# Four weight splits and the columns moved in a fused two-block kernel's beginning, column sums closed by kind, splits and turnings moved in its last mixer

## The reference, cut to what matters

```
m_lat = silu(c)     @ ada_w[i] + ada_b[i]      # 6 parts of 1024: shift, scale, gate, twice
m_ctx = silu(c_ctx) @ ada_w[i] + ada_b[i]
h = rms_norm(x) * (1 + scale) + shift
x = x + gate * rms_norm(mixer(h));  x = x + gate * rms_norm(relu(h' @ w1)**2 @ w2)
```

```
s   = (q @ k.T) * exp(logd - m_t)              # logd: decays, masked
num = s @ v + w_inter * (q @ C);  den = sum(s) + w_inter * (q @ n)
out = num / max(|den|, exp(-m_t))              # then directions added, RMS norm by head
y   = (sigmoid(o) * out * norm_w) @ w_out
```

## Time and profile before

| | us |
|---|---|
| median of 3 runs (lowest, highest) | 2018.97 (2018.01, 2020.7) |
| profiled execution, its own time | 2022.0 |
| its span, first to last instruction | 2020.2 |
| TensorE busy | 1967.8 |
| VectorE busy | 1359.3 |
| ScalarE busy | 886.4 |
| mean granted TensorE clock | 0.989 |

### The profile page before, as it was taken

How to read it: one execution, slowest core, us unless ns; L and a number is a source line. 1 busy time by engine, 2 the same in 40 slices (tenths; PEclk the granted TensorE clock), 3 DMA queues, 4 the chain that set the end, 5 groups by cost and what they waited for, 6 DMA issues and landing times.

```text
span 2020.2 us, 27551 instructions
## 1 busy us (share of the span) xinstructions
PE 1967.8 (97%) x10390; PEld 1643.3 (81%) x10390; DVE 1359.3 (67%) x2172; ACT 886.4 (44%) x1513; POOL 254.4 (13%) x333
## 2 busy tenths in 40 slices
PE   7899999999999999999999999999999999989998
PEld 3777788888888777888998888878888878878897
DVE  4778777777756645487987675667655477667655
ACT  2523345232333544476554224624243354556554
POOL 2101011111110210411101000111011021331000
PEclk9889999999999999999999999999999999999999
DMA  8334226565664261258874432555555345236753
GB/s 290 117 100 119 90 70 212 188 178 159 193 181 139 93 201 53 83 185 284 262 229 139 156 105 71 188 170 168 152 168 165 86 133 179 89 101 217 229 184 114
DMA packets 191859, 315.20 MB, mean 156 GB/s; under 512 B 14653, under 2 KB 114328, under 8 KB 191728
## 3 DMA queue, kind: packets, MB, share of 16 engines
q1 hardware_dynamic: 162512, 210.09, 32.4%
q0 software_dynamic: 29216, 103.36, 17.1%
HBM read 312.35 MB, written 1.05 MB: 155 GB/s over the span
## 4 chain that ended last, share of the span: by engine, by line
PE 89%; DVE 4%; issue 2%; ACT 2%; POOL 1%; DMA 1%; SPq 0%; POOLq 0%; DVEq 0%; ACTq 0%
PE bank L676 26%; PE bank L683 24%; PE bank L682 24%; PE bank L686 11%; PE bank L681 2%; PE bank L679 2%; ACT junk L1556 1%; PE bank L745 1%; DVE wl L2153 1%; POOL st L3140 1%; DVE X L2275 0%; PE bank L1045 0%; DVE acc L2178 0%; ACT wh L1540 0%; ACT ta L1584 0%
## 5 line engine op out<-in xcount | busy, mean ns | idle before, releaser
L1540 ACT ACTIVATE wh<-raw 128x1024 fp32r<-128x1024 f32 (+4 forms) x390 | 399.3, 1030 | 602.0 <-PE bank L683 564.1
L2153 DVE TENSOR_TENSOR wl<-raw,wh 128x1024 fp32r<-128x1024 f32 (+3 forms) x372 | 440.0, 1189 | 297.3 <-ACT wh L1540 296.8
L676 PE MATMUL bank<-HH,wh 128*128 128x256 f32 (+1 forms) x1552 | 517.1, 333 | 2.8 <-issue 2.1
L682 PE MATMUL bank<-HL,wh 128*128 128x512 f32 (+1 forms) x1232 | 415.0, 337 | 0.0
L683 PE MATMUL bank<-HH,wl 128*128 128x512 f32 (+1 forms) x1232 | 415.0, 337 | 0.0
L2178 DVE SCALAR_TENSOR_TENSOR acc<-ada,sc,acc 128x512 f32<-128x512 f32 x518 | 362.3, 746 | 2.3
L676 PEld LDWEIGHTS bank<-HH,wh 128*128 128x128 f32 x1552 | 294.8, 190 | 32.5 <-issue 6.4
L676 PE MATMUL bank<-wh,UH 128*128 128x512 f32 x768 | 302.3, 394 | 0.0
L683 PE MATMUL bank<-wh,UL 128*128 128x512 f32 x768 | 301.4, 393 | 0.0
L682 PE MATMUL bank<-wl,UH 128*128 128x512 f32 x768 | 301.0, 392 | 0.0
L682 PEld LDWEIGHTS bank<-HL,wh 128*128 128x128 f32 x1232 | 232.0, 188 | 28.1 <-issue 2.2
(11 more groups left out here) (342 smaller groups left out, 2602.9 us busy)
## 6 DMA issues: line engine op xcount, KB each, us to landing
raw<-in_mlp_w SPq DMA_DIRECT2D x256, 512.0 KB, 4.1
ada<-in_mod_w POOLq DMA_DIRECT2D x96, 512.0 KB, 4.7
ada<-in_ada_w POOLq DMA_DIRECT2D x80, 512.0 KB, 4.5
raw<-in_ml_w_qkvo SPq DMA_DIRECT2D x28, 512.0 KB, 4.1
raw<-in_conv_w_in SPq DMA_DIRECT2D x24, 512.0 KB, 4.5
raw<-in_ada_w SPq DMA_DIRECT2D x12, 512.0 KB, 6.0
raw<-in_mla_w_o SPq DMA_DIRECT2D x8, 512.0 KB, 3.9
raw<-in_gla_w_v SPq DMA_DIRECT2D x8, 512.0 KB, 3.7
```

Source lines behind the costliest of these rows:

```text
L676: pe.matmul(o, sh, mh, start=start, stop=False, skip_group_check=True)
L682: pe.matmul(o, sh, ml, start=False, stop=False, skip_group_check=True)
L1540: act.activation(k.wh[n % NSPL][:, 0:m], k.raw[(NDIRECT + n) % NRAW][:, 0:m], ACT.Copy).then_inc(*k.w_hi.up("w hi", n))
L2153: dve.tensor_tensor(k.wl[n % NSPL][:, 0:m], k.raw[(NDIRECT + n) % NRAW][:, 0:m], k.wh[n % NSPL][:, 0:m].bitcast(F32), ALU.subtract).then_i ...
```

## The change

Six edits, all in the order of work; no instruction of another kind is added.

1. `Walk.step`: the end of a shift or scale unit with two kinds becomes two ends, the first kind after 3 units, the second after 4, each with its own bank. The accumulator is free after the second.
2. Beginning: ACT and DVE cut four blocks ahead of the second group of evictions, the first of them ahead of `make(0, 0, 1, ...)`; rows 2 and 3 are prepared behind the direct columns. POOL only counts.
3. PE: `last_columns` stands amid the second block, behind its first two tiles, and no more ahead of the third.
4. Heads: ACT's `take` moves from the end of even steps to odd ones (from 3), between the exponential (and the gate's eviction) and `back`.
5. Heads: PE's `normed` at 8, 12, 15 (from 7, 11, 15); DVE's `gated` at 9, 13, `gated_low` at 10, 14; ACT's `gated_high` at 9, 13.
6. Layer 1 to 2: DVE's last cut of the transition stands before the last tile's residual and no more behind its rows.

```diff
--- before.py
+++ after.py
@@ -316,7 +316,11 @@
         for c in self.closing:
             c[0] -= 1
         self.flush(0)
-        if end is not None:
+        if end is not None and end[0] == "finish" and end[2] not in (2, 5) and len(end[4]) == 2:
+
+            self.closing.append([self.lag, key, end[:4] + ((0,), False)])
+            self.closing.append([self.lag + 1, key, end[:4] + ((1,), end[5])])
+        elif end is not None:
             self.closing.append([self.lag, key, end])
 
     def flush(self, limit):
@@ -722,14 +726,15 @@
                     mm(b[:, :], k.ones[:], k.acc[:, n % 2, ty, :]).then_inc(*b.filled())
                     ps.give(b)
             else:
-                b = ps.take("mod", li, part, ch)
+                b = ps.take("mod", li, part, ch, types[0])
                 w.wait_ge(*b.before())
                 for i, ty in enumerate(types):
                     for m in range(4):
                         p = mm(b[:, i * 4 + m:i * 4 + m + 1], k.acc[:, n % 2, ty, m * 128:m * 128 + 128], k.ones[:, 0:1])
                 p.then_inc(*b.filled())
                 ps.give(b)
-            at.put(("acc used", n), b.full())
+            if types[-1] == 1:
+                at.put(("acc used", n), b.full())
 
     walk = Walk(len(k.blocks), split, unit, close)
 
@@ -842,6 +847,8 @@
                 n = walk.take()
                 wh, wl = block_ready(n)
                 for t in tiles:
+                    if (kk, t) in among:
+                        among[kk, t]()
                     w.wait_ge(*bs[t].before())
                     o = (t - off) * 128
                     for q in range(2):
@@ -956,7 +963,7 @@
     def mla(last_columns):
         ready = hidden_ready(0, 0)
 
-        proj_tok(("cq",), HHL, [0, 1, 2, 3], ready, nhs=(0,), width=384, among={2: last_columns})
+        proj_tok(("cq",), HHL, [0, 1, 2, 3], ready, nhs=(0,), width=384, among={(1, 2): last_columns})
 
         def turned(f):
             wd = 128 if f < 5 else 64
@@ -1438,7 +1445,7 @@
                 gate_part(j - 2)
             if j:
                 back(*steps[j - 1])
-            if j in (7, 11, 15):
+            if j in (8, 12, 15):
                 normed((j - 7) // 4)
         gate_part(14)
         back(*steps[-1])
@@ -2080,14 +2087,16 @@
             front(h, r)
             if j in (5, 9, 13):
                 o_out((j - 5) // 4)
+            if j >= 3 and j % 2:
+                walk.take()
             if j:
                 back(*steps[j - 1])
             if h and r:
                 over_den(h - 1)
                 head_squares(h - 1)
-            if j in (8, 12):
-                gated_high((j - 8) // 4)
-            if j < 2 or j % 2 == 0:
+            if j in (9, 13):
+                gated_high((j - 9) // 4)
+            if j < 2:
                 walk.take()
         back(*steps[-1])
         walk.take()
@@ -2111,14 +2120,16 @@
 
     prep(0, 0, 0, [at("x0", 0)] * 2)
     direct_out(0, 0)
-    for t in range(1, 3):
+    prep(0, 0, 1, [at("x0", 1)] * 2)
+    direct_out(0, 1)
+    for t in range(2, 4):
         prep(0, 0, t, [at("x0", t)] * 2)
-    direct_out(0, 1)
-    prep(0, 0, 3, [at("x0", 3)] * 2)
-    for hf in range(2):
-        make(0, 0, hf, range(0, 2))
+    make(0, 0, 0, range(0, 2))
+    walk.cut_next()
+    make(0, 0, 1, range(0, 2))
     walk.cut_next()
     direct_out(1, 0)
+    walk.cut_next()
     walk.cut_next()
     make(0, 0, 0, range(2, 4))
     make(0, 0, 1, range(2, 4))
@@ -2223,7 +2234,7 @@
                                              op1=ALU.mult).then_inc(*k.gate_rows.up())
                 at.put(("gate rows", li, part, ch), k.gate_rows.last())
             else:
-                b = ps.of("mod", li, part, ch)
+                b = ps.of("mod", li, part, ch, types[0])
                 done = columns_out(li, part, b, ch * 4, [b[:, i * 4:i * 4 + 4] for i in range(2)], types)
                 if li == 0 and part < 2:
                     at.put(("mod half", part, ch), done)
@@ -2402,13 +2413,16 @@
         residual(li, part, 2)
         walk.cut_next()
         prep(nli, which, 2)
+        if not which:
+            walk.cut_next()
         walk.ensure((nli, 3 * which), (nli, 3 * which + 1))
         y_out(li, part)(1, 3)
         gated(li, part, 3)
         residual(li, part, 3)
         walk.cut_next()
         prep(nli, which, 3)
-        walk.cut_next()
+        if which:
+            walk.cut_next()
         pending.append((nli, which, allowed))
 
     def rest():
@@ -2978,10 +2992,10 @@
             if j in (6, 10, 14):
                 means((j - 6) // 4)
                 normed((j - 6) // 4)
-            if j in (8, 12):
-                gated((j - 8) // 4)
             if j in (9, 13):
-                gated_low((j - 9) // 4)
+                gated((j - 9) // 4)
+            if j in (10, 14):
+                gated_low((j - 10) // 4)
         walk.take()
         back(*steps[-1])
         over_den(7)
@@ -3019,18 +3033,19 @@
     w.wait_ge(*b.full())
     dve.tensor_copy(k.gcol[:], b[:, 0:5]).then_inc(*b.emptied())
     direct_out(0, 0)
-    prep(0, 0, 2)
     direct_out(0, 1)
-    prep(0, 0, 3)
+    for t in range(2, 4):
+        prep(0, 0, t)
     make(0, 0, 0, range(0, 2))
     unit(("add", 0, 1, 1, 2, (0, 1)))
-    make(0, 0, 1, range(0, 1))
     walk.cut_next()
-    make(0, 0, 1, range(1, 2))
+    make(0, 0, 1, range(0, 2))
     walk.cut_next()
     unit(("add", 0, 1, 1, 3, (0, 1)))
+    walk.cut_next()
     direct_out(1, 0)
     close(("finish", 0, 1, 1, (0, 1), False))
+    walk.cut_next()
     make(0, 0, 0, range(2, 4))
     make(0, 0, 1, range(2, 4))
     walk.allow((0, 3), (0, 4), (0, 2))
@@ -3299,8 +3314,8 @@
         prep(0, 0, t)
 
     w.wait_ge(*at("raw", NDIRECT))
-    walk.cut_next()
-    walk.cut_next()
+    for _ in range(4):
+        walk.cut_next()
     walk.allow((0, 3), (0, 4), (0, 2))
 
     mixers = (mla, gla, conv, mlstm)
```

## The result

The changed kernel takes 2027.25 us in the median of 7 runs (2025.56 to 2029.21), the kernel before, run beside it, 2019.49 (2018.01 to 2022.41): a ratio of 1.0038 with a 95% interval of 1.0026 to 1.0049, **about 7.8 us slower** where 7.8 us faster was forecast. The profiled execution took 2027.97 us, its span is 2026.1.

The account below looks back on a forecast made before the run. TensorE, busy 97% of the span, was taken as the bound, with VectorE setting the pace in the heads. Beginning -8.6, column sums -4.5 and heads +5.3 gave -7.8: from 2018.97 to 2011.2 us, range 2003.5 to 2017.5.

Parts of the forecast that it names:

- Seven steps by 0.95 us = 6.6 lost: Last mixer's heads: ScalarE's weight split, moved ahead of the scaled product, delays VectorE's addition; net loss 5.3 us, ends 0 and 7.
- what counts is ScalarE's order: Last mixer's heads: VectorE sets the pace, so only where ScalarE's split stands matters, with a loss of 5.3 us.
- The upper end of 7 for the heads: Last mixer's heads: largest loss expected, 7 us, with bank waits at the shifted turnings of half a microsecond a cycle.
- So moving the turnings and the gating one step later removes TensorE waits that nobody downstream waits for: 0.: Last mixer's heads: removing TensorE's waits gains 0 us, because VectorE sets the pace.
- Beginning, 8.6: First projections: an earlier start and no wait before the third weight block gain 8.6 us, 10.9 at best.
- TensorE needs it only after the first two tiles: First projection: the second hidden pair, ready at 37.8, is needed only at 38.8, so TensorE starts at 36.7.
- the two losses: Beginning: lower clock costs 1.6 us in blocks 0 and 1, 1.8 in blocks 2 and 3; two thirds, 2.3 us, kept.
- The next wait: Behind the beginning, TensorE's turning of normed rows: slack falls from 4.2 to 3.0 us, so none of the gain is lost.
- Column sums by kind, 4.5: Closing column sums kind by kind removes a low-clock stretch behind the group at 99.96: gain 4.5 us, ends 0 and 5.1.
- The argument from the clock row: Column sums: no other group of sixteen is followed by a low-clock stretch, held against rival (a), 2015.7 us, chance 0.18.
- Rival (d): Heads: more waits bring TensorE to half clock, up to +31.5 us, 2037 us in all; chance 0.05.
- The low end of the terms: Whole kernel: best beginning, clock back and heads neutral were said to give 2002 us.

Follow-up runs that it names:

- fourteenth: The changed kernel with edit 5 undone and, in the heads, GpSimd's low half held until its step's head sum: 2018.3 us, ratio 0.9987 to the kernel before.
- fourth: The changed kernel with edits 4 and 5 undone, so the heads are as before: 2011.6 us, ratio 0.9956 to the kernel before.
- thirteenth: The changed kernel with edit 5 alone undone, low halves not held: 2025.1 us, ratio 1.0025 to the kernel before.
- twelfth: The best version (2009.6 us) with GpSimd's last low half of the heads held until the last head sum: 2010.6 us, ratio 0.9949 to the kernel before.

## Why the prediction was wrong

By differences of neighbouring kernels the 7.7 us are: edits 2, 3 and 6 -4.8; edit 1 beside them -4.1; the split's delay +6.3 (fourteenth less fourth); the low half over the head sums +7.6 (thirteenth less fourteenth); edit 5 +2.7 (changed kernel less thirteenth). Each of these has an interval of about 2 to 3.6 us to either side. The traces divide it nearly alike: -6.7 ahead of the heads, then +4.5, +7.7 and +2.0, in all +7.5.

- **Heads, "Seven steps by 0.95 us = 6.6 lost", loss 5.3.** Right as far as it goes: +4.4 alone and +6.3 in the changed kernel by the times, 4.6 and 4.5 by the traces, with the addition waiting 0.83 us. The step that failed is what stands around it: "what counts is ScalarE's order". The split has a second half on GpSimd, released by the first, and the prediction counted only the instruction that the diff moves. That half came to lie over the head sum, +7.6. The upper end of 7 for the heads was therefore too low by 7 (traces, 14.2) to 10 us (times, 16.6).
- **"So moving the turnings and the gating one step later removes TensorE waits that nobody downstream waits for: 0."** The runs show no gain from these waits, as it said. The move itself was not free: +7.3 alone, of which 4.7 was the gated subtraction under GpSimd's low half; in the changed kernel, where the low half has left that place, +2.7, with bank waits of up to 4.7 us.
- **Beginning, 8.6.** A size, off by a wrong step: "TensorE needs it only after the first two tiles". The code waits for both halves ahead of the first tile. TensorE started at 37.7, 1.0 us late. The other 1.8 us are clock: of the two losses the prediction kept 2.3 us, and the changed kernel had about 4.1, as the first 36 matmuls took 8.0 us instead of 6.2 and the rest of the projection 2.3 more than at full clock. 5.7 us were gained in the trace, 4.8 in the times. With the wait by tile the first 36 took 6.5 us in all three traces that have it; with the old wait and the new beginning they took 8.0 in six of seven traces and 6.4 in one. The next wait gave nothing back, as forecast: the normed rows were ready at 70.5, and turned at 73.41.
- **Column sums by kind, 4.5.** The number was met beside the new beginning (4.1, roughly 0.5 to 7.7) and missed by the edit alone (0.6). The step behind it failed: it took the low stretch of one execution for the code's own and ascribed it to the group of sixteen. The unchanged code shows it in two of six traces. That the number was met once may be luck. The argument from the clock row, that behind other groups it stands at 9, was too coarse as well: in the trace before the clock is 0.83 from 880 to 900, and the slice over it reads 9.
- **The sum.** The forecast was -7.8, of which the edits of the beginning and of the columns were to give 13.1; they gave 8.9. The heads were to take 5.3, and took 16.6 by the times, 14.2 by the traces. Rival (d) had the sign, but not the mechanism: the clock over the changed kernel's heads is still 0.94. The low end of the terms comes to 2018.97 - 10.9 - 5.1 = 2003.0, not 2002, which changes nothing above. Edit 6 was never run by itself; it is in the 4.8.

## What to carry to other kernels

When an instruction is moved, follow its releases to the other engines' queues: what starts when it ends moves along, and may land on something. Before moving work of GpSimd or under it, list VectorE's instructions whose operands all lie in SBUF, and look in the trace for any that already takes longer than its likes; one such row (2.26 us for 0.62) gave this away before the change. Such a row counts as busy, so no list of waits shows it. A gap that an edit should close is worth checking against the waits in the code, operand by operand. And a stretch at the lower clock that an edit is to remove should be looked for in several executions first.

The best version found keeps the new beginning and the column sums by kind, leaves the heads as they were, and waits for hidden halves by tile: 2009.6 us, 0.5% below the kernel before.

## What the runs showed of the hardware

- GpSimd's low half (2.38 us, two operands in SBUF) stops a VectorE instruction with two operands in SBUF until it ends: 2.86 us for 0.68, 2.85 for 0.69, 2.47 for a pair of 0.62. The order of starting decides, and a chain of it can be read in the kernel before. GpSimd's gate starts first, and the multiplication of the normed heads (0.69 us when nothing lies over it) takes 1.10. The multiplication is then the first, and GpSimd's low half, started at 1791.29, ends 2.25 us behind the multiplication's end at 1791.87, so it took 2.83 instead of 2.38:

```profile
1790.71 0.62 POOL L3270 TENSOR_SCALAR m_so<-m_so 128x512 f32<-128x512 f32 x1
1790.77 1.10 DVE L2939 TENSOR_TENSOR Y<-Y 128x512 f32<-128x512 f32 x1 [1.12 <-POOL Y L3265]
1791.29 2.83 POOL L3068 TENSOR_TENSOR wl<-raw,wh 128x1024 fp32r<-128x1024 f32 x1
```

- VectorE's instructions with one operand in a bank kept their times under it (m_D 0.69, the additions 0.43, tp 0.87 for two), but in the twelfth a `TENSOR_SCALAR` of 128x4 with its one operand in SBUF did not (1.60 for 0.17). The same section of the Trainium skill's page "SBUF — State Buffer" names that case too: copies, casts and `tensor_scalar` can enter two-port modes, in which they contend with GpSimd. The row agrees in its length; no row shows the mode.
- The same code in the same order can run through a stretch at full clock in one execution and at half in another: the window from 100 to 115 had a mean clock of 0.66 in two traces and of 1.00 in four, with TensorE busy throughout in both. It costs 4.9 us where it comes (16.5 us for 11.7).
